# Modulation vectors from a transposed weight by dot products on VectorE, shift and scale loaded row block by row block

## What is computed

```python
def rms_norm(x, g):
    y = x * rsqrt(mean(x * x) + EPS)
    return y * g

def first_block(x, c, w_ada, b_ada, g_mix, w_in):
    ...
    mod = jax.nn.silu(c) @ w_ada[layer] + b_ada[layer]
    sh1, sc1, gt1, sh2, sc2, gt2 = jnp.split(mod, N_MOD, axis=-1)

    h = modulate(rms_norm(x, g_mix[layer]), sh1, sc1)      # h * (1 + sc1) + sh1
    proj = h @ w_in[layer]
    q_sb, k_sb, v_sb, q_d, k_d, v_d, gate_sb, gate_d = jnp.split(proj, splits, axis=-1)
    o_sb = stick_breaking_attention(q_sb, k_sb, v_sb)      # 8 heads of 64
    o_d = dilated_attention(rope(q_d), rope(k_d), v_d)     # 12 heads in 3 groups
    merged = sigmoid(gate_sb) * (o_sb @ w_sb_o) + sigmoid(gate_d) * (o_d @ w_dil_o)
    x = x + gt1 * (merged @ w_out)

    h2 = modulate(rms_norm(x, g_ffn), sh2, sc2)
    x = x + gt2 * peer_ffn(h2, w_pq, peer_keys, peer_u, peer_v)   # 8 heads, top 16 of 16,384 experts
    return rms_norm(x, g_final)
```

## Time and profile before

| | us |
|---|---|
| median of 3 executions | 1,408.63 (1,407.36 to 1,409.34) |
| the profiled execution | 1,407.81 |
| its span | 1,405.9 |
| TensorE busy | 1,280.6 (91%) |
| VectorE busy | 782.3 (56%) |
| ScalarE busy | 329.2 (23%) |
| GpSimd busy | 303.0 (22%) |
| bytes moved | 519.37 MB, mean 369 GB/s |

### The profile page before, as it was taken

How to read it: one execution, slowest core, us unless ns; L and a number is a source line. 1 busy time by engine, 2 the same in 40 slices (tenths; PEclk the granted TensorE clock), 3 DMA queues, 4 the chain that set the end, 5 groups by cost and what they waited for, 6 DMA issues and landing times.

```text
span 1405.9 us, 14584 instructions
## 1 busy us (share of the span) xinstructions
PE 1280.6 (91%) x4834; PEld 729.0 (52%) x4834; DVE 782.3 (56%) x2096; ACT 329.2 (23%) x863; POOL 303.0 (22%) x275
## 2 busy tenths in 40 slices
PE   7999999999998997879889989898986799999998
PEld 6787995566555553434335444444432244544444
DVE  6257547777766775786747585665556542220002
ACT  2321223432311131232212212111110043311102
POOL 0000004333433232333222232231433000000000
PEclk7999999999999999999999999999999999999999
DMA  9998889999999999999999999999999998678882
GB/s 387 414 326 302 297 311 363 382 420 418 418 419 418 419 384 418 415 363 418 417 416 405 417 386 417 405 418 416 414 417 417 380 413 312 212 253 292 286 300 94
DMA packets 102313, 519.37 MB, mean 369 GB/s; under 512 B 12000, under 2 KB 12768, under 8 KB 67424
## 3 DMA queue, kind: packets, MB, share of 16 engines
q0 software_dynamic: 38592, 293.62, 51.1%
q1 hardware_dynamic: 61200, 219.31, 41.7%
q10 hardware_dynamic: 2448, 5.51, 1.1%
HBM read 515.77 MB, written 1.05 MB: 368 GB/s over the span
## 4 chain that ended last, share of the span: by engine, by line
PE 37%; DMA 14%; DVE 4%; issue 1%; ACT 1%; ACTq 0%; DVEq 0%
PE ps_M L968 26%; DMA ring<-in_w_second 12%; PE ps_T L770 3%; PE ps_T L771 3%; DMA ring<-in_peer_uv,arena 2%; DVE hT L2320 1%; DVE ring L2101 1%; PE ps_OT L956 1%; PE ps_SA L739 1%; PE ps_SA L1025 1%; PE ps_T L956 1%; PE ps_M L984 0%; PE ps_S L997 0%; PE ps_SA L1037 0%; DVE arena L2020 0%
## 5 line engine op out<-in xcount | busy, mean ns | idle before, releaser
L968 PE MATMUL ps_M<-ring,arena 128*128 128x512 f32 x1072 | 490.7, 597 | 42.7 <-DMA ring<-in_w_second 41.9
L968 PEld LDWEIGHTS ps_M<-ring,arena 128*128 128x128 f32 x1072 | 194.9, 190 | 281.4 <-issue 218.1
L1275 POOL DMA_INDIRECT ring<-in_peer_uv,arena x137 | 158.0, 1153 | 332.9 <-PE ps_T L771 298.4
L1275 POOL DMA_INDIRECT arena<-in_peer_uv,arena x105 | 123.1, 1172 | 239.2 <-PE ps_T L771 217.7
L770 PE MATMUL ps_T<-ring,arena 128*128 128x512 f32 x230 | 123.1, 617 | 27.1 <-ACT arena L1414 27.0
L1403 ACT ACTIVATE arena<-arena 128x2 f32<-128x2 f32 x128 | 25.9, 202 | 437.9 <-DVE arena L2121 421.5
L771 PE MATMUL ps_T<-ring,arena 128*128 128x512 f32 x230 | 119.9, 603 | 0.0
L2101 DVE SCALAR_TENSOR_TENSOR ring<-ring,merged 128x1024 f32<-128x1024 f32 x72 | 87.7, 1222 | 48.1 <-DMA ring<-in_peer_uv,arena 47.9
L770 PE MATMUL ps_T<-arena 128*128 128x512 f32 x178 | 94.6, 614 | 20.6 <-ACT arena L1414 19.4
L2101 DVE SCALAR_TENSOR_TENSOR ring<-ring,arena 128x1024 f32<-128x1024 f32 x65 | 79.2, 1220 | 31.3 <-DMA ring<-in_peer_uv,arena 29.9
L771 PE MATMUL ps_T<-arena 128*128 128x512 f32 x178 | 92.8, 603 | 0.0
(11 more groups left out here) (312 smaller groups left out, 1508.9 us busy)
## 6 DMA issues: line engine op xcount, KB each, us to landing
ring<-in_w_second SPq DMA_DIRECT2D x274, 512.0 KB, 4.5
ring<-in_w_in SPq DMA_DIRECT2D x66, 512.0 KB, 9.3
arena<-in_w_ada POOLq DMA_DIRECT2D x12, 2048.0 KB, 11.3
ring<-in_w_pq SPq DMA_DIRECT2D x28, 512.0 KB, 6.1
ring<-in_w_out SPq DMA_DIRECT2D x16, 512.0 KB, 5.0
ring<-in_w_br SPq DMA_DIRECT2D x16, 384.0 KB, 3.7
ring<-in_peer_uv,arena POOLq DMA_INDIRECT x137
arena<-in_w_in SPq DMA_DIRECT2D x4, 512.0 KB, 8.7
```

Of the source, the lines that this page charges most:

```text
L968: m = mm(bank, left[c], w[:, c, :], start=first and c == 0, stop=last and c == 1)
L1275: pool.indirect_dma_start(row_slots[s], None, A["peer_uv"], bass.IndirectOffsetOnAxis(ap=expert[:, u % 3, k:k + 1], axis=0))\
```

## The change

w_ada is laid out transposed on the host: 48 blocks of 128 outputs, each 128 partitions (the outputs) x 1,024 inputs. silu(c) is spread as a row over all partitions (`silu_row`: c by a broadcast DMA, tanh on ScalarE, one operation on VectorE), and one operation of VectorE with an accumulator gives 128 outputs as a column, which is the form in which they are used. TensorE has no part in it any more; the ones columns and their bank are gone.

The first sublayer's shift and scale come as 16 single blocks on SP's queue, between the stick tiles; after the two blocks of a row block VectorE finishes that row block's shift and gain, and ScalarE writes it to hT. The stick tiles run accordingly: tiles 0 to 3 over row blocks 0 to 2, then tiles 4 to 7 over row blocks 0 to 2, then all eight for each further row block. The squares are added in pairs of row blocks before the matmuls with ones. Chunks 4 to 11 still come by POOL, 2 MB each, now in pieces of 4 KB instead of 16 KB; chunk 4 is used behind the stick softmax instead of ahead of it, and each further chunk one place later. Masks follow the v tiles on SP's queue.

```diff
--- before
+++ after
@@ slots and tensors @@
-        ada_sum = carve(3, 512)
+        silu_row = carve(D)
...
-        ada_slots = [arena[:, lo:lo + KC * 512].rearrange("p (c n) -> p c n", n=512)
+        ada_slots = [arena[:, lo:lo + KC * 512].rearrange("p (b k) -> p b k", k=D)
                      for lo in (at_rows, at_rows + KC * 512, at_gate, at_dil)]
...
+        c_tanh = hT[:, 0:4, :].rearrange("p c t -> p (c t)")
...
-        w_ada_v = A["w_ada"].rearrange("t p (c n) -> t p c n", c=KC)
+        w_ada_v = A["w_ada"].rearrange("b p k -> p b k")
@@ TensorE @@
-            def stick_half(i, half):
+            def stick_part(i, c):
...
-                for c in range(4 * half, 4 * half + 4):
-                    if i == 0:
-                        pe.wait_ge(h_norm1, c + 1)
-                    m = mm(ps[b][:, lo:lo + T], w[:, c, :], hT[:, c, :], start=i % 2 == c == 0, stop=i % 2 == 1 and c == KC - 1)
+                pe.wait_ge(h_norm1, c + 1)
+                m = mm(ps[b][:, lo:lo + T], w[:, c, :], hT[:, c, :], start=i % 2 == c == 0, stop=i % 2 == 1 and c == KC - 1)
...
-            def ada_columns(ch):
...
-            for c in range(KC):
-                pe.wait_ge(sq_ready, c + 1)
-                m = mm(bank[:, 0:T], ones[:, :], tmp[:, c, :], start=c == 0, stop=c == KC - 1)
+            pe.wait_ge(squares_ready, 1)
+            for c in range(KC // 2):
+                m = mm(bank[:, 0:T], ones[:, :], tmp[:, c, :], start=c == 0, stop=c == KC // 2 - 1)
...
+            for c in range(3):
+                for i in range(4):
+                    stick_part(i, c)
+            for i in range(4, 8):
+                for c in range(3):
+                    stick_part(i, c)
+            for c in range(3, KC):
+                for i in range(8):
+                    stick_part(i, c)
@@ SyncE @@
-            for dst, n in ((tri, "tri"), (stick_neg, "stick_neg")):
-                eng.dma_start(dst, K[n]).then_inc(const_in, 16)
+            eng.dma_start(silu_row, A["c"].partition_broadcast(P)).then_inc(c_in, 16)
...
+            def first_blocks(c):
+                for s in range(2):
+                    eng.dma_start(ada_slots[c // 2][:, 2 * (c % 2) + s, :], w_ada_v[:, KC * s + c, :]).then_inc(first_in[s][c], 16)
+
+            first_blocks(0)
+            first_tiles(0, 4)
+            first_blocks(1)
+            first_blocks(2)
+            first_tiles(4, 8)
+            for c in range(3, KC):
+                first_blocks(c)
+            first_tiles(8, 12)
+            for dst, n in ((tri, "tri"), (stick_neg, "stick_neg")):
+                eng.dma_start(dst, K[n]).then_inc(const_in, 16)
@@ GpSimd @@
-            for ch in CHUNKS[:4]:
-                pool.dma_start(ada_slots[ch], w_ada_v[ch]).then_inc(ada_in[ch], 16)
...
-                pool.dma_start(ada_slots[ch % 2], w_ada_v[ch]).then_inc(ada_in[ch % 2], 16)
+                pool.wait_ge(ada_used, 4 * (ch - 3) if ch < 6 else 16 + 4 * (ch - 5))
+                pool.dma_start(ada_slots[ch % 2], w_ada_v[:, 4 * ch:4 * ch + 4, :]).then_inc(ada_in[ch % 2], 16)
@@ ScalarE @@
+            for c in range(0, KC // 2, 2):
+                F(tmp[:, c:c + 2, :], xT[:, c:c + 2, :], ACT.Square).then_inc(squared, 1)
+            act.wait_ge(c_in, 16)
+            F(c_tanh, silu_row, ACT.Tanh, scale=0.5).then_inc(silu_half, 1)
...
@@ VectorE @@
+            def mod_dot(slot, at, b, weight):
+                w = ada_slots[slot][:, at, :]
+                V.scalar_tensor_tensor(w, w, weight, silu_row, ALU.mult, ALU.mult, accum_out=modT[:, b:b + 1]).then_inc(ada_used, 1)
+
+            def first_dots(c):
+                for s, weight in ((0, 0.5), (1, half_gain[:, c:c + 1])):
+                    dve.wait_ge(first_in[s][c], 16)
+                    mod_dot(c // 2, 2 * (c % 2) + s, KC * s + c, weight)
+
             def ada_chunk(ch):
+                dve.wait_ge(ada_in[ch % 2], 16 * (ch // 2 - 1))
+                for n in range(4):
+                    mod_dot(ch % 2, n, 4 * ch + n, 0.5)
...
+                V.tensor_tensor(modT[:, bs], modT[:, bs], b_ada_col[:, bs], ALU.add).then_inc(mod_ready, 1)
...
+            for c in range(KC):
+                V.tensor_tensor(tmp[:, c, :], xT[:, c, :], rstd[:, :], ALU.mult).then_inc(st.tick(), 1)
+                if c > 0:
+                    first_dots(c)
+                dve.wait_ge(ada_used, 2 * c + 2)
+                own()
+                V.tensor_tensor(first_mod[:, :, c], first_mod[:, :, c], first_base[:, :, c], ALU.add).then_inc(scaled, 1)
@@ host @@
-    x["w_ada"] = column_tiles(x["w_ada"][0], 512)
+    x["c"] = x["c"].reshape(D)
+    x["w_ada"] = x["w_ada"][0].T.reshape(6 * KC, P, D)
```

178 lines of the change are left out of this document (43 added, 135 removed).

## The result

The changed kernel takes 1,398.84 us (median of 5 runs, 1,397.93 to 1,402.43), the kernel before 1,409.34 us in the same comparison (5 runs, 1,407.36 to 1,410.19). The ratio is 0.993, with a 95% interval of 0.991 to 0.9949: faster by 0.7%. The forecast was 1,393.5 us in a range of 1,388 to 1,402. Sign and range hold. Of the forecast gain of 15.2 us, 10.5 came by these medians and 9.15 by the two profiled executions (1,407.81 us before, 1,398.66 after).

What follows compares the result with a forecast made beforehand. TensorE was taken to bound the kernel up to the first gather, transfers from there. Terms 10.6 - 0.6 + 4.0 + 1.2 = 15.2 us off 1,407.8, plus 0.8, gave 1,393.5 us, range 1,388 to 1,402.

Steps and rivals of the forecast that it cites:

- Bound and propagation: TensorE bounds up to the first gather, transfers behind it; time gained ahead moves everything behind by the same amount.
- the rival that it would not propagate: The gather stretch starts earlier but ends as before: 1,404 to 1,409 us, chance 4%.
- the halving: VectorE's dots: two fp32 SBUF sources might halve throughput, 2.45 us a dot, 1,420 us in all; chance 3%.
- E, 10.6 forecast: End of the opening's stick matmuls on TensorE: from 59.0 to 48.4 us, a gain of 10.6 us.
- TensorE is the bound with 3 us in hand: Opening, row 7: data there at 41.8 us, TensorE reaches it at 44.9, so TensorE sets the end.
- dq0, "loss 0.6 us": Tile dq0, behind the opening: its load lands at 58.3 us, TensorE wants it at 57.7, a loss of 0.6.
- POOL's chunks overtake: Behind the opening: chunks 4 and 5 take three quarters, v tiles and masks land late: 1,396.5 us, chance 15%.
- my own list: The forecast's signs of being wrong, among them dq0's matmuls waiting more than 2 us.
- The stretch from 60 to 195 us, 4.0 forecast: Between opening and tail: five groups of ada columns (chunks 5 to 9) leave TensorE, gaining 4.0 us.
- 5 x 0.81, all on the bound: Chunks 5 to 9: each group of columns takes TensorE 0.81 us, all counted as gain, 4.0 us.
- nothing, thin: Chunk 11 ahead of the merges: costed at nothing with thin cover; worst landing gives a stall of 0.1 us.
- The tail, "gain 1.2 us": Ahead of the first query: without chunks 10 and 11's columns it ends near 200.1 instead of 201.3 us.

Runs made afterwards that it cites:

- run 3: Changed kernel plus 28 unused 128-column matmuls on TensorE in the opening, 14 ahead of the norm's matmuls and 14 behind: 1,396.62 us.
- run 4: Changed kernel plus four unused 128-column matmuls ahead of the first query: 1,396.65 us.
- run 1: Changed kernel with POOL waiting for tile dq0's landing before it issues chunks 4 and later: 1,392.26 us, ratio 0.9889.
- run 2: Changed kernel with the peer keys (1 MB) loaded behind twelve more tiles: 1,395.39 us.
- run 5: Changed kernel plus eight unused one-column matmuls where chunks 10 and 11 had their columns before: 1,402.1 us.
- run 6: Changed kernel plus four unused one-column matmuls at each of the five old places of chunks 5 to 9: 1,403.36 us.
- run 9: Changed kernel with chunks 4 and later held until dq0 landed, peer keys twelve tiles later, four unused 128-column matmuls ahead of the first query: 1,393.02 us.
- run 12: The changed kernel again, unedited: 1,399.16 us.
- run 8: Kernel before with one four-column matmul for each of chunks 4 to 11 instead of four one-column ones: 1,404.62 us.
- run 11: Changed kernel with chunks 4 and later held until dq0 landed, and three unused 128-column matmuls ahead of the first query: 1,390.63 us, ratio 0.9872.
- run 10: Changed kernel with stick tiles and SP's loads back in two halves, and chunks 4 and later held until dq0 landed: 1,397.91 us.
- run 7: Changed kernel with stick tiles in two halves as before and SP's loads in that order, dots kept: 1,397.96 us.

## Why the prediction was right, and where it was not

**Bound and propagation**: right. The stretch behind the first gather stays between 1,191.3 and 1,197.0 us, whether the gather starts at 195.5 or at 212.0 us; the rival that it would not propagate is out. VectorE's dots took 1,206 to 1,227 ns, 40 of them, against 1.22 forecast, with fresh weights in the slots (the eight whose scalar is the gain took 1.28):

```profile
L1835 DVE SCALAR_TENSOR_TENSOR arena<-arena x40: 1206/1221/1227, 10.5 to 158.8; 128x1024 f32<-128x1024 f32 x40
```

So the halving that the Trainium skill (Vector Engine (DVE) Microarchitecture Reference, Points that are easy to get wrong) names for two non-bf16 sources in SBUF did not come on top of the row, as I had weighed it.

**E, 10.6 forecast, 10.0 measured**: right in size, but not by the path of the sum, and in part by luck. "TensorE is the bound with 3 us in hand" was right at row 7 (ready at 42.35, used at 45.3) and wrong at row 3, where the sum had data at 29.0 and TensorE at 30.7. Row 3's copy ended at 30.83, and data and TensorE met within 0.7 us (run 3). The sum let row 3's first dot run before both blocks had landed at 26.8; its block was there only at 27.41:

```profile
27.41 1.23 DVE L1835 SCALAR_TENSOR_TENSOR arena<-arena 128x1024 f32<-128x1024 f32 x1 [4.25 <-DMA arena<-in_w_ada]
```

Three smaller errors ran the other way: VectorE's pace was 2.88 us a row block, not 3.2; eight records of the last 40 matmuls took 1.73 us from start to start, not 1.77; and the slow rows ended at about 25 us, as I had put it, in the changed kernel and run 4, but in runs 1, 2, 5, 6, 9 and 12 only row 0 was slow. There the data of row 3 set E, at 48.3 to 48.5.

**dq0, "loss 0.6 us"**: the failed term; measured 6.0 together with the clock. The mechanism was right (bytes queued ahead of a tile whose slot comes free late), size off. The rate was 402 to 404 GB/s from 5 to 62 us, not 415: 22.1 MB take 1.6 us more. I counted the bytes ahead of dq0 as if nothing behind it moved; by 62.4 us 24.03 MB had, 0.9 MB of them for later tiles, 2.3 us. Together 58.3 + 3.9 = 62.2, measured 62.46. And the wait took the clock with it, 1.76 us, which the sum had at nothing and no row of before showed. The traffic of 37 to 62 us by queue (packets, MB, share of 16 engines; q1 is SP's, q0 POOL's):

```profile
q1 hardware_dynamic: 2193, 5.90, 60.7%
q0 software_dynamic: 1048, 4.17, 42.0%
```

The 4.17 MB of q0 are chunks 4 and 5, whose first dot runs at 70.42 us; they are a part that could go (run 1), and the peer keys another (run 2). The Trainium skill (DMA: Bandwidth & Descriptors, Issuing engines are not separate DMA queues) says that loads started by different engines run on the same 16 DMA engines and interleave with each other; the trace agrees, 60.7 and 42.0% side by side. The rival "POOL's chunks overtake" named the right bytes but the wrong victim: the v tiles and masks came in time, dq0 did not. By my own list (a wait of dq0's matmuls for more than 2 us) this was the place to look.

**The stretch from 60 to 195 us, 4.0 forecast, 5.6 measured**: the term "5 x 0.81, all on the bound" was right for the changed kernel (run 6: 4.2) and wrong for the kernel before (run 8), so that it came near is partly luck. Three of the five groups lay ahead of a wait of 1.32 us for a chain with VectorE's chunk in it. I named VectorE's shorter chunk and put no price on it. It removed that wait, 1.3 us beyond the columns, in this execution wholly (0.2 to 0.5 us of it were there in runs 1, 4, 9, 11 and 12), and without it the three groups would have given nothing. Chunk 11's cover of "nothing, thin" held, and it was thin: the dots waited 8.76 us for their load, the bias ended at 160.22 and the first merge began at 160.26. That is 0.48 us behind TensorE's matmul for it, where it was 0.12 before, and TensorE did not yet wait.

```profile
155.35 1.23 DVE L1835 SCALAR_TENSOR_TENSOR arena<-arena 128x1024 f32<-128x1024 f32 x1 [8.76 <-DMA arena<-in_w_ada]
...
160.06 0.16 DVE L1850 TENSOR_TENSOR modT<-modT,vecT 128x4 f32<-128x4 f32 x1
160.26 0.42 DVE L1951 SCALAR_TENSOR_TENSOR arena<-arena,ps_M 128x256 f32<-128x256 f32 x1
```

In run 9, where TensorE came to the merges 6 us earlier, it no longer held (0.7 us of waiting), and in run 11 0.3.

**The tail, "gain 1.2 us"**: wrong in sign, -0.65, in two parts. First, the data: ScalarE's rows came hardly earlier without the columns (2.22 us behind the norm's matmuls instead of 2.32), and the query needs the last of them. With the clock at 1.00 the stretch takes 5.30 to 5.32 us (runs 4, 9, 10 and 11) against 5.81 before, so only 0.5 us was to be had. I had let the query take 2.05 us from the start of the first row; it takes 2.33 to 2.44 and begins 0.64 us behind it in run 10. Second, the clock: a wait of 0.81 us opened ahead of the query, and at the lower level the query takes 1.2 us more. Matmuls ahead of it bring this back (run 4; 5.31 us in runs 9 and 11 too). What decides in each case stays open: with the wait of 0.81 us the clock fell in seven executions (after the change, and in runs 1, 2, 3, 6, 7 and 12) and not in run 10; with columns and no wait it fell in run 5 and not in the kernel before; in run 8, with two four-column matmuls and a wait of 0.47 us, it stayed up. The Trainium skill (TensorE: Matmul & The Clock Gate, What's actually happening) says that the monitor's timing runs free of the kernel, so that the place of a transition varies; runs 7 and 10, and the two executions of the changed kernel, agree with that, though none of them tests it.

The sum 1,407.8 - 15.2 + 0.8 is 1,393.4, not 1,393.5; nothing hangs on it.

## What to carry to other kernels

When an opening gets shorter, everything that was hidden behind it is wanted earlier: list the loads in the order in which they are wanted, with their bytes, those of other queues and those behind them too, and hold back whatever is wanted later (here 1 MB ahead of the tile cost 2.6 us of waiting). A work item removed from the bounding engine gains only up to the next wait on its path; look at which engine's chain ends that wait, and price the change's effect on that chain as well. Put a price on the clock for each new wait of TensorE, both at half speed behind it and without.
